# Four products ahead of the norm: the first gate, up and input projections take X times the norm weight and are scaled by the inverse root afterwards

## The reference

```python
def rms_norm(x, w):
    xf = x.astype(jnp.float32)
    y = xf * lax.rsqrt(jnp.mean(xf * xf, axis=-1, keepdims=True) + EPS)
    return (y * w.astype(jnp.float32)).astype(x.dtype)

def swiglu(x, w_gate, w_up, w_down):
    return (jax.nn.silu(x @ w_gate) * (x @ w_up)) @ w_down

x = x + 0.5 * swiglu(rms_norm(x, ffn1_norm), ffn1_w_gate, ffn1_w_up, ffn1_w_down)
h = rms_norm(x, mix_norm)
proj = h @ w_in                                   # 1024 -> 3600
qkv_a, z_a, a_a, b_a, qkv_b = jnp.split(proj, split_at, axis=-1)
o_a = gdn_mixer(qkv_a, z_a, a_a, b_a, ...)        # short convolution of 5 taps first
o_b = dilated_mixer(qkv_b, ...)
x = x + jnp.concatenate([o_a, o_b], axis=-1) @ w_out
x = x + 0.5 * swiglu(rms_norm(x, ffn2_norm), ffn2_w_gate, ffn2_w_up, ffn2_w_down)
x = rms_norm(x, final_norm)                       # then the two other blocks
```

## Time and profile before

| | |
|---|---|
| median of three runs | 2711.52 us (2707.78 to 2720.34) |
| the profiled execution itself | 2705.44 us |
| span in the trace | 2703.0 us |
| PE busy / DVE / ACT / POOL | 96% / 63% / 40% / 3% |
| mean granted TensorE clock | 0.988 |
| chain that ended last, PE's share | 88% |

### The profile page before, as it was taken

How to read it: one execution, slowest core, us unless ns; L and a number is a source line. 1 busy time by engine, 2 the same in 40 slices (tenths; PEclk the granted TensorE clock), 3 DMA queues, 4 the chain that set the end, 5 groups by cost and what they waited for, 6 DMA issues and landing times.

```text
span 2703.0 us, 38913 instructions
## 1 busy us (share of the span) xinstructions
PE 2602.5 (96%) x15924; PEld 2304.3 (85%) x15924; DVE 1692.1 (63%) x2681; ACT 1085.1 (40%) x1687; POOL 69.6 (3%) x64
## 2 busy tenths in 40 slices
PE   7998898999999999999999999999999999998998
PEld 6998778999888888778888888889888888888998
DVE  6767644677767655656644677655555456776664
ACT  5445642545422223334243422324223225555543
POOL 0001032000000000000010000000000000000000
PEclk9999899999999999999999999999999999999999
DMA  6665200476455543112223355543444333244454
GB/s 246 234 224 189 87 14 24 167 245 213 148 187 180 180 155 107 57 43 68 97 86 102 122 189 172 181 161 118 139 140 132 133 103 125 74 131 158 166 193 148
DMA packets 110113, 380.98 MB, mean 141 GB/s; under 512 B 12016, under 2 KB 17392, under 8 KB 109552
## 3 DMA queue, kind: packets, MB, share of 16 engines
q1 hardware_dynamic: 108928, 373.32, 41.6%
q10 hardware_dynamic: 1008, 5.18, 0.5%
HBM read 377.40 MB, written 1.05 MB: 140 GB/s over the span
## 4 chain that ended last, share of the span: by engine, by line
PE 88%; DVE 5%; ACT 4%; issue 2%; DMA 0%; ACTq 0%; SPq 0%; DVEq 0%
PE B L1457 25%; PE B L1459 25%; PE B L1458 25%; ACT w_hi L1778 2%; DVE w_lo L2074 2%; PE B L1717 1%; PE B L1700 1%; PE B L1472 1%; PE B L1610 1%; PE B L1473 1%; PE B L1474 1%; PE B L1624 1%; PE B L1617 1%; PE B L1707 1%; DVE AC L2320 1%
## 5 line engine op out<-in xcount | busy, mean ns | idle before, releaser
L1457 PE MATMUL B<-U,w_hi 128*128 128x256 f32 (+1 forms) x2896 | 961.6, 332 | 9.4 <-DVE w_lo L2074 5.5
L1458 PE MATMUL B<-U,w_hi 128*128 128x256 f32 (+1 forms) x2896 | 952.1, 329 | 0.0
L1459 PE MATMUL B<-U,w_lo 128*128 128x256 f32 (+1 forms) x2896 | 951.9, 329 | 0.0
L2074 DVE TENSOR_TENSOR w_lo<-w_raw,w_hi 128x1024 fp32r<-128x1024 f32 (+3 forms) x587 | 684.7, 1178 | 411.2 <-ACT w_hi L1778 410.3
L1778 ACT ACTIVATE w_hi<-w_raw 128x1024 fp32r<-128x1024 f32 (+3 forms) x587 | 591.2, 1013 | 502.8 <-PE B L1459 478.5
L1457 PEld LDWEIGHTS B<-U,w_hi 128*128 128x128 f32 x2896 | 547.1, 189 | 66.6 <-issue 10.8
L1458 PEld LDWEIGHTS B<-U,w_hi 128*128 128x128 f32 x2896 | 546.9, 189 | 53.5 <-issue 2.2
L1459 PEld LDWEIGHTS B<-U,w_lo 128*128 128x128 f32 x2896 | 546.8, 189 | 51.4
L1457 PE MATMUL B<-HHf,w_hi 128*128 128x256 f32 (+1 forms) x1122 | 363.9, 324 | 1.8 <-DVE w_lo L2074 1.8
L1459 PE MATMUL B<-HHf,w_lo 128*128 128x256 f32 (+1 forms) x1122 | 363.0, 324 | 0.0
L1458 PE MATMUL B<-HLf,w_hi 128*128 128x256 f32 (+1 forms) x1122 | 363.0, 324 | 0.0
(11 more groups left out here) (351 smaller groups left out, 2620.7 us busy)
## 6 DMA issues: line engine op xcount, KB each, us to landing
w_raw<-in_w SPq DMA_DIRECT2D x504, 512.0 KB, 4.2
w_ada<-in_w SPq DMA_DIRECT2D x144, 512.0 KB, 3.4
w_raw<-in_w SPq DMA_DIRECT2D x58, 384.0 KB, 3.2
w_raw<-in_w SPq DMA_DIRECT2D x16, 240.0 KB, 2.5
X<-in_x SPq DMA_DIRECT2D x2, 1024.0 KB, 9.7
w_raw<-in_w SPq DMA_DIRECT2D x8, 256.0 KB, 2.6
BW<-in_bias ACTq DMA_DIRECT2D x1, 1536.0 KB, 10.3
K<-in_consts ACTq DMA_DIRECT2D x2, 640.0 KB, 5.6
```

What stands on the lines that cost most here:

```text
L1457: pe.matmul(o, hi, xh, start=i == 0 and s.start, stop=False)
L1458: pe.matmul(o, hi, xl, start=False, stop=False)
L1459: e = pe.matmul(o, lo, xh, start=False, stop=i == last and s.stop)
L2074: dve.tensor_tensor(w_lo[:, plan.slot[u], 0:n], w_raw[:, plan.ring[u], 0:n], w_hi[:, plan.slot[u], 0:n].bitcast(F32), ALU.subtract).then_i ...
```

## The change

Before each of the three norms a second set of high and low parts is written, of X times the norm weight, without the root: step `plain` on ACT (one activation with the weight as its scale) and `plain_lo` on DVE. For `mix_norm` and `ffn2_norm` these follow each row's last addition into X. The new function `border` replaces norm and `pair`: four products (gate and up of rows 0 and 1, or the convolution inputs 0 to 3) run on the plain parts, in four quarters of 24 matmuls. The sums over partitions stand between the first and the second quarter. The normed parts are written beside them, for all later products. The four banks are multiplied by the root when they are read: `ffn_r` and `conv_r`, on DVE. The additions of squares of the first and third norm (`sq_pool`) and three of eight low parts (`norm_lo` with `s.arg`) go to GpSimd. The silu of the conditioning vector `CS` and its DMA move behind the first border and the first weights.

```diff
+    def border(self, name, keys, pieces, x, stat, wait_u, *scaled, a=None):
+        if not a:
+            self.add("plain_lo", key=(name, 7), x=x)
+        need, banks = tuple(("pl", (name, k)) for k in range(8)), [self.PS.get() for _ in range(4)]
+        a = a or self.fetch(pieces[:16])
+        for i in range(4):
+            if i == 2:
+                a = self.weights(pieces[16:])
+            self.add("pair", ... wts=a[8 * (i % 2):8 * (i % 2) + 8], x=x, n=256, ... k0=4 * (i % 2), need=need)
+            if not i:
+                rb = stat.rsqrt(D)
+                norms = self.norm_to_u(name, rb, wait_u, *scaled)
+            else:
+                for _ in range((0, 5, 3, 0)[i]):
+                    next(norms, None)
...
+            elif k == "plain":                                       # ACT
+                act.activation(HI[s.x][:, s.key[1], 0:256], X[:, s.key[1], 0:256], ACT.Copy, scale=col(*s.key))
...
+            elif k == "plain_lo":                                    # DVE
+                dve.scalar_tensor_tensor(out=LO[s.x][...], in0=X[...], scalar=col(*s.key), in1=HI[s.x][...], op0=ALU.mult, op1=ALU.subtract)
+            elif k == "ffn_r":
+                dve.tensor_tensor(TM(s.t, 256), PS(s.b, 256), RB(s.rb, 256), ALU.mult)
+                dve.tensor_tensor(TM(s.t2, 256), PS(s.b2, 256), RB(s.rb, 256), ALU.mult)
+            elif k == "conv_r":
+                dve.tensor_tensor(CV[:, s.key, 2:258], PS(s.b, 256), RB(s.rb, 256), ALU.mult)
...
+        self.sum = "sq_pool" if name in ("x", "wout") else "sq_add"
...
-        sp.dma_start(CS[:].rearrange("p v k -> p (v k)"), ...)
         for u in plan.cut[:NR]:
             sp.dma_start(w_raw[:, plan.ring[u], 0:plan.units[u][1]], source(u))
+        sp.dma_start(CS[:].rearrange("p v k -> p (v k)"), ...)
```

More of the change, by code:

```diff
@@ L411, in down, with ffn @@
         return [(p + "d", k, 128 * m, 128) for k in range(NF)]
-    def ffn(self, p, n, begun, gate, old, stat=None, beside=None):
+    def ffn(self, p, n, begun, gate, old, stat=None, beside=None, then=None, rb=None):
         turns, share = 0, lambda i: min(i * ADA[p] // ADAS[p], ADA[p])
@@ L420, in ffn @@
             t = self.TM.get()
-            self.add("ffn_h", key=(p, j), n=n, b=g, b2=u, t=t, need=old)
-            self.PS.done(g, ("silu", (p, j)))
-            self.PS.done(u, ("hm", (p, j)))
+            if rb and j < 2:
+                t2 = self.TM.get()
+                self.add("ffn_r", key=(p, j), b=g, b2=u, t=t, t2=t2, rb=rb)
+                self.add("ffn_h", key=(p, j), n=n, t=t, t2=t2, need=old)
+                self.PS.done(g, ("gr", (p, j)))
+                self.PS.done(u, ("ur", (p, j)))
+                self.TM.done(t2, ("hm", (p, j)))
+            else:
+                self.add("ffn_h", key=(p, j), n=n, b=g, b2=u, t=t, need=old)
+                self.PS.done(g, ("silu", (p, j)))
+                self.PS.done(u, ("hm", (p, j)))
             self.TM.done(t, ("hl", (p, j)))
@@ L453, in whole @@
[L453 to L463, removed]
@@ L464, in whole @@
-        begun = dict(zip(keys, self.pair(keys, wts, 256, need)))
+        f1, f2 = [[(p, x, j) for j in range(2) for x in "gu"] for p in ("f1", "f2")]
+        scaled = lambda p: [(e, (p, j)) for e in ("gr", "ur") for j in range(2)]
+        rb, banks = self.border("ffn1_norm", f1, self.first_two("f1"), "UO", stat, None, *scaled("f1"), a=a)
+        self.add("cs")
+        x = lambda m: self.plain("mix_norm", m, "UO", ("mm", ("f1", "u", 1)), ("x_add", ("f1", "d", m)))
+        stat = self.ffn("f1", 256, dict(zip(f1, banks)), None, (), then=x, rb=rb)
@@ new lines, in whole @@
+        win = [("win", k, 128 * j, 128) for i in range(2) for k in range(8) for j in (2 * i, 2 * i + 1)]
+        rb, banks = self.border("mix_norm", [("in", j) for j in range(4)], win, "UO", stat, self.lastU,
+                                *(("conv_r", j) for j in range(4)))
+        rc, stat = self.mix1(rb, banks)
+        self.view = "UO"
+        rb, banks = self.border("ffn2_norm", f2, self.first_two("f2"), "U0", stat, ("mm", ("wout", 7)), *scaled("f2"))
+        begun = dict(zip(f2, banks))
@@ L528, in conv @@
         def conv(j):
-            if j > 1:
+            if j < 4:
+                self.add("conv_r", key=j, b=first[j], rb=rb, need=(old,))
+                PS.done(first[j], ("conv_r", j))
+                yield ("D", 420),
+            else:
                 yield from PS.room()
[L531 to L534, removed]
+                b = self.gemm(("in", j), win(128 * j), 256)
+                self.add("conv_in", key=j, b=b, need=(old,))
+                PS.done(b, ("conv_in", j))
+                yield split + (("P", 2750), ("A", 380))
             self.add("conv_taps", key=j, need=(old,))
@@ L1118, in settle @@
             i = self.i - 1
-            before = ("sq", (self.name, 0)) if i == 1 else ("sq_add", (self.name, i - 1))
-            self.p.add("sq_add", key=(self.name, i), n=self.w, t=self.late, need=(before,))
-            self.p.TM.done(self.late, ("sq_add", (self.name, i)))
+            before = ("sq", (self.name, 0)) if i == 1 else (self.sum, (self.name, i - 1))
+            self.p.add(self.sum, key=(self.name, i), n=self.w, t=self.late, need=(before,))
+            self.p.TM.done(self.late, (self.sum, (self.name, i)))
             self.late = None
@@ L1834, in scalar @@
                 p, j = s.key
-                w.wait_ge(*at("mm", (p, "g", j)))
-                w.each(s.t.after)
-                act.activation(TM(s.t, s.n), PS(s.b, s.n), ACT.Silu).then_inc(*up("silu", s.key))
+                if s.t2:
+                    w.wait_ge(*at("gr", s.key))
+                    act.activation(TM(s.t, s.n), TM(s.t, s.n), ACT.Silu).then_inc(*up("silu", s.key))
+                else:
+                    w.wait_ge(*at("mm", (p, "g", j)))
+                    w.each(s.t.after)
+                    act.activation(TM(s.t, s.n), PS(s.b, s.n), ACT.Silu).then_inc(*up("silu", s.key))
                 w.wait_ge(*at("hm", s.key))
```

105 lines of the change are left out of this document (79 added, 26 removed).

## The result

| | before | changed |
|---|---|---|
| median, same chip, in turns | 2710.22 us (2707.78 to 2720.34, 4 runs) | 2732.31 us (2730.74 to 2737.37, 4 runs) |
| ratio | | 1.0077, 95% interval 1.0059 to 1.0094 |
| profiled execution, its span | 2705.44, 2703.0 | 2732.75, 2730.7 |

The kernel became 0.8% slower. I had forecast no change, and 2732 lies above my range. The page of the changed kernel has the same shares of time and a longer span, with 21.5 us more of PE time for the same 15924 matmuls; its slices of 68 us show no stage that stands out.

A forecast was written before the change was run, and what follows sets the result against it. PE was taken to bound the kernel nearly everywhere. Start +2.0, mixers +1.3 and second feed-forward layer -2.6 made +0.7 us, so a forecast median of 2712 us (no change that can be told), range 2697 to 2724.

The forecast's parts named there:

- 2.0 slower: Start: stalls of 4.7 us for late weight units against 2.7 us gained on the first four products.
- The three large waits: Start: PE waits 3.8 us for GpSimd's sum, 0.7 for the sixth weight unit and 3.1 for the eighth.
- the two small ones: Start: stalls of 0.3 and 0.6 us at the two weight units after the eighth.
- my bound of 1.8 gained: Start, best case: GpSimd's additions fully hidden, sum ready at 18.3, all behind it 3.8 us earlier.
- 0.9 us ahead of the old kernel: Mixers' border: PE waits 3.6 us for `CB` and goes on at 226.0, against 226.9 for the old order.
- I take 1.2 off: Mixers' stage: moving out c2 and c3, filler of 5.44 us, loses 1.2 us of their gain.
- the filler worth nothing gives 5.5 lost: Mixers, worst case: taking c2 and c3 out of the later stage returns nothing, 5.5 us lost.
- rival (d): Mixers' stage answers to DVE, where `conv_r` now stands, and loses 5.5 us: 2717 us; chance 0.1.
- forecast 7.9: Before f2: four products done at 500.0 against 507.9; after 5.4 us of stalls, net 2.6 faster.
- (b): First norm's sum and borders' low parts: GpSimd and DVE hinder each other, 14 us slower, 2726; chance 0.1.
- (a): All three borders: weight units keep pace with PE, 15.1 us faster, 2696; chance 0.15.
- (c): Mixers: `CB` lands in time or PE bounds them after all, 4 to 6 us faster than the sum, 2707; chance 0.2.

The follow-up runs named there:

- e1: Kernel before with only the border at the program's start as in the changed kernel; ratio to before 1.0017.
- e7: The changed kernel run once more, nothing changed in it; ratio to before 1.0074.
- e2: Kernel before with only the border before the mixers as in the changed kernel; ratio to before 1.0056.
- e4: As e2, but the four scaled evacuations come right away and the taps of c2, c3 wait for the fourth attention product's way out; ratio to before 1.0044.
- e8: The changed kernel, all three borders, with the mixers' evacuations and taps ordered as in e4; ratio to before 1.0042.
- e11: As e2, but all four scaled evacuations come right away; the taps of c2 and c3 stay ahead on DVE; ratio to before 1.0057.
- e13: Kernel before with c2 and c3 moved right behind c0 and c1 in the mixers' order, no border changed; ratio to before 1.0043.
- e3: Kernel before with only the border before f2 as in the changed kernel; ratio to before 1.0000.
- e9: The kernel before run once more, nothing changed in it; stage from f1's end to the delta rule 131.7 us, against 132.9.
- e10: As e8, plus the start's sums of squares on DVE and the DMAs of the mixers' constants issued ahead of the border; ratio to before 1.0093.

## Why the prediction was wrong

**Start: nearly right, one term left out.** I said 2.0 slower. At equal pace f1 ends at 206.5 (e1) and 207.3 (e7), against 202.8 to 204.0 in eight traces with the old start, mean 203.5: 3.0 to 3.8 slower. GpSimd's sum came 0.7 later than forecast, and still the four products ended on time. The three large waits are there within 0.7 us; the two small ones (0.3 and 0.6) are not. What I left out is the clock behind the wait for the eighth unit: 24 matmuls took 1.6 more there. I had charged a low clock behind GpSimd's sum and not behind this wait. (And my bound of 1.8 gained does not follow from its own numbers: a sum ready at 18.3 and not at 20.0 moves what follows by 1.7, which is 0.3 slower.)

**Border of the mixers: right, on the good side by 1.2.** I had the matrix of v begin 0.9 us ahead of the old kernel. It begins 22.0 us after f1's end with four products done; before 18.7 with two, and two are 5.4: 2.1 ahead. `CB` is waited for 1.1 and not 3.6, and the 1.0 that I charged for the clock behind it was 0.2 (48 matmuls of v in 11.54 us, before 11.35).

**The mixers' stage behind it: wrong, and this is the error.** The step was "5.44 taken out of a stage with 14.9 idle returns less than 5.44. I take 1.2 off", with "the filler worth nothing gives 5.5 lost" as its bound. From v's begin to the delta rule the old trace needs 114.3 and the changed one 122.6, with 5.4 less to do: 13.8 lost instead of 1.2. The bound was no bound. It counts what the two products could cover; but they were a cover in one place, and when the planner lost them it also moved eight taps, 4.0 us of DVE, ahead of a link of the attention chain. Over the traces the stage grew from 130.9 to 145.5, the mean of the changed kernel's two and e2: 14.6. e2 shows the loss alone. e4 and e8 take 7 to 12.5 us of stage back with the order mended, 9.4 of it against e11 by DVE's order alone. e13 loses 4 to 6 for the cover with no border changed, which is about what e4 keeps (135.2 against 130.9). The rival (d), the stage answering to DVE, named the right engine, with 5.5 of the 14.6 and a chance of 0.1; but it blamed `conv_r`, and e11 and e4 both have that and differ by the taps.

A part of the stage is not waiting but PE's busy time, 4.8 more with the same matmuls and about the same granted clock. The changed kernel's row, which stands against the 114.36 of before:

```profile
212.80:357.42 144.62, 119.20 (x808) 105.04 (x806) 93.30 (x210) 81.09 (x162) 14.49 (x13) 0.93 0.35 127
```

Two thirds of it are the 32 small matmuls that read `QB` (line 1536 before, 1590 now), 3.2 us more. These are their busy times in the stage, before and changed, and one group of them in each:

```profile
203.08:336.01 132.93, 4.56 (x32) 0.92 0.39 138
212.80:357.42 144.62, 7.74 (x32) 0.93 0.35 127
255.13 1.14 PE L1536 MATMUL B<-QB 64*128 64x256 f32 x8
261.76 1.13 PE L1590 MATMUL B<-QB 64*128 64x256 f32 x4
```

Each uses 64 partitions. The even heads have the lower 64 and the odd ones the upper. The eight of an even and an odd head, one behind the other, take 1.14; the four of one head alone take 1.13. Before, all four pairs of heads stand together. Now two pairs are torn apart by other matmuls of the new order, and one of their fours took 2.0, behind the wait of 2.3, at a granted clock of 0.50. The other 1.6 stay open.

**Border of f2: mechanism right, half the size.** Four products end 14.0 us after wout, before 21.7: 7.7 ahead, forecast 7.9. The waits are 1.43, 1.22 and 1.50 (1.2, 1.5 and 1.8). Two small stalls that I had charged (0.3 and 0.6) are not there. In their place the fifth product takes 0.8 longer, for its late rows, which I had not charged. From wout's end to f2's first down matmul it is 128.65 against 129.98, in e3 128.3: 1.3 to 1.7 gained, not 2.6. The four products and the waits add up to more than this, and not all of the rest is found.

**Rivals.** (b) fell as put: the twelve additions took 721 to 745 ns, none 1.5 us. The cost that it feared was on DVE, and small: eight instructions beside GpSimd took 0.95 to 0.97 instead of 0.48, 4 us of DVE in all three borders together. (a) fell, the units did not keep pace. (c) holds for `CB`, 1.1 instead of 3.6, and was paid away behind it. The sum with measured sizes, 3.4 + 14.6 - 1.5 = 16.5 us, lies at the low end of what the ratio allows, 16 to 25. The 4 to 5 us between it and the medians stay open; a slower pace that comes more often with all three borders would be one cause, and of the right size. The single trace's 27.7 is 3.4 + 6.3 (f1's pace) + 11.7 + 2.5 - 1.3 + 5.1; the 2.5 (delta rule to wout) and the 5.1 (behind f2) are in code that is the same, and e1, which changes only the start, shows 2.5 and 3.6 of them. From the delta rule to wout the trace of before took 150.6, and e9, the same kernel, 152.8, as 15 of the 17 traces do within 0.5: the 2.5 are luck of that one trace.

## What to carry to other kernels

When products are moved forward, ask what they covered where they were and what a planner now puts in their place: price the chain that loses its cover, not the length of the cover. Look through the new order for long blocks on an in-order engine (here 4 us of taps) that have come ahead of a short step someone waits for; e11 and e4 differ in nothing else. Look also at what stood side by side and is now apart. And where single executions differ by more than the effect, measure a change part by part at landmarks, with one trace of unchanged code beside it.

## What the runs showed of the hardware

A dense run of 128x256 matmuls goes at 113.3 or at 117.8 ns each, at a granted clock of 1.00 in both, and keeps its pace for up to 1584 matmuls, until a pause. The same code shows both in different executions; one run at the slower pace costs 6 to 7 us here.

The same wait of 2.85 us was followed by a granted clock of 0.66 over 5 us in e1 and of 1.00 in e5.

Eight matmuls of 64 partitions, four on the lower half and four on the upper, took 1.14 us, as long as four on one half alone.

GpSimd and DVE hindered each other by very different amounts. Six sums on GpSimd at the start took 0.72 to 0.745 us, as alone, but two low parts of DVE beside them took 0.96 and 0.95 instead of 0.48 (the last line gives line 2146's shortest, median and longest in ns):

```profile
15.47 5.08 POOL L2547 TENSOR_TENSOR SSB<-SSB,TMP 128x256 f32<-128x256 f32 x6 [15.03 <-ACT TMP L1837]
...
14.36 3.02 DVE L2146 SCALAR_TENSOR_TENSOR U<-X,PC,U 128x256 fp32r<-128x256 f32 x5
...
L2146 DVE SCALAR_TENSOR_TENSOR U<-X,PC,U x24: 476/479/959, 8.3 to 515.9; 128x256 fp32r<-128x256 f32 x24
```

The split took 1.93 instead of 1.22 beside the bias sums, and in e10 eight taps took 7.64 instead of 4.00. The Trainium skill (SBUF — State Buffer, Who interferes with whom) says that a DVE instruction with two inputs in SBUF contends with a GpSimd instruction that reads SBUF. The taps and these low parts read both inputs there, and their near doubling agrees. The sums at the start show the cost on DVE only.
